# Two transformer blocks on one core: the last additions to x moved from the engines into accumulating transfers of GpSimd's queue

## The reference

```python
def second_block(x, ...):
    ...
        x = x + rms_norm(merged @ w_out[l], norm_mix_post[l])

        h = rms_norm(x, norm_ffn_pre[l])
        u = causal_dwconv(h @ w_up[l], conv_ffn_w[l])
        a, g = jnp.split(u, 2, axis=-1)
        f = (jax.nn.gelu(g, approximate=True) * a) @ w_down[l]
        x = x + rms_norm(f, norm_ffn_post[l])
    return x
```

## Time and profile before

| | us |
|---|---|
| median of 3 runs | 1413.34 |
| lowest and highest of them | 1412.82, 1951.74 |
| profiled execution, its own time | 1412.42 |
| profiled execution, its span | 1411.1 |
| PE busy in the span | 1362.0 |
| mean granted TensorE clock, share of full speed | 0.993 |

### The profile page before, as it was taken

The page is one execution under the profiler, slowest core; times in us unless marked ns, Lnnn a source line. Parts: engine busy times, 40 slices in busy tenths (PEclk is TensorE's granted clock), DMA queues, the critical chain, the costliest instruction groups (busy, mean ns, idle before and its releaser), DMA issues.

```text
span 1411.1 us, 17413 instructions
## 1 busy us (share of the span) xinstructions
PE 1362.0 (97%) x7040; PEld 1123.8 (80%) x7040; DVE 759.7 (54%) x1082; ACT 603.9 (43%) x866; POOL 7.0 (0%) x15
## 2 busy tenths in 40 slices
PE   5999998989999999999999999999989999999997
PEld 3777876878888888889888888788987888888886
DVE  5678855575555443335524444345767666563224
ACT  5646866453333333223334544334524443443221
POOL 0000000000000000000000000000000000000000
PEclk9999999999999999999999999999999999999998
DMA  9743321323332223323232121234302333323331
GB/s 382 274 136 135 128 72 57 129 78 138 143 135 94 100 86 98 95 82 103 79 101 75 60 75 47 75 106 146 106 16 80 100 92 106 101 86 98 95 95 60
DMA packets 43102, 150.45 MB, mean 107 GB/s; under 512 B 4752, under 2 KB 6928, under 8 KB 41872
## 3 DMA queue, kind: packets, MB, share of 16 engines
q1 hardware_dynamic: 42144, 144.76, 30.8%
q0 software_dynamic: 880, 4.59, 1.0%
HBM read 146.45 MB, written 2.10 MB: 105 GB/s over the span
## 4 chain that ended last, share of the span: by engine, by line
PE 87%; DVE 8%; ACT 3%; issue 2%; DMA 1%; DVEq 0%; SPq 0%; ACTq 0%
PE banks L580 26%; PE banks L582 25%; PE banks L581 25%; ACT w_hi L1321 1%; DVE w_lo L1871 1%; PE banks L865 1%; PE banks L724 1%; PE banks L732 1%; PE banks L721 1%; PE banks L1127 1%; PE banks L1126 1%; PE banks L848 1%; PE banks L694 1%; PE banks L1118 1%; PE banks L1154 1%
## 5 line engine op out<-in xcount | busy, mean ns | idle before, releaser
L580 PE MATMUL banks<-h_lo,w_hi 128*128 128x512 f32 (+1 forms) x1248 | 473.6, 380 | 13.1 <-DVE h_lo L2513 5.6
L582 PE MATMUL banks<-h_hi,w_hi 128*128 128x512 f32 (+1 forms) x1248 | 470.0, 377 | 0.0
L581 PE MATMUL banks<-h_hi,w_lo 128*128 128x512 f32 (+1 forms) x1248 | 469.3, 376 | 0.0
L1871 DVE TENSOR_TENSOR w_lo<-raw_w,w_hi 128x1024 fp32r<-128x1024 f32 (+2 forms) x221 | 256.2, 1161 | 322.2 <-ACT w_hi L1321 319.9
L1321 ACT ACTIVATE w_hi<-raw_w 128x1024 fp32r<-128x1024 f32 (+2 forms) x221 | 221.4, 1004 | 235.1 <-PE banks L582 210.1
L580 PEld LDWEIGHTS banks<-h_lo,w_hi 128*128 128x128 f32 x1248 | 234.3, 188 | 65.8 <-issue 10.5
L581 PEld LDWEIGHTS banks<-h_hi,w_lo 128*128 128x128 f32 x1248 | 234.5, 188 | 43.5
L582 PEld LDWEIGHTS banks<-h_hi,w_hi 128*128 128x128 f32 x1248 | 234.4, 188 | 42.4
L582 PE MATMUL banks<-a_hi,w_hi 128*128 128x512 f32 (+1 forms) x396 | 146.2, 369 | 0.0
L581 PE MATMUL banks<-a_hi,w_lo 128*128 128x512 f32 (+1 forms) x396 | 145.8, 368 | 0.0
L580 PE MATMUL banks<-a_lo,w_hi 128*128 128x512 f32 (+1 forms) x396 | 145.6, 368 | 0.0
(11 more groups left out here) (315 smaller groups left out, 1516.9 us busy)
## 6 DMA issues: line engine op xcount, KB each, us to landing
raw_w<-in_w_ffn_up SPq DMA_DIRECT2D x44, 512.0 KB, 3.4
raw_w<-in_w_up SPq DMA_DIRECT2D x44, 512.0 KB, 3.4
raw_w<-in_ada_rows SPq DMA_DIRECT2D x24, 512.0 KB, 4.2
early<-in_ada_turned SPq DMA_DIRECT2D x8, 1024.0 KB, 16.6
raw_w<-in_w_gates SPq DMA_DIRECT2D x16, 512.0 KB, 3.2
raw_w<-in_w_ffn_down SPq DMA_DIRECT2D x16, 448.0 KB, 3.3
raw_w<-in_w_down SPq DMA_DIRECT2D x16, 448.0 KB, 3.3
raw_w<-in_w_conv SPq DMA_DIRECT2D x12, 512.0 KB, 3.3
```

The source lines that it names most:

```text
L580: e.matmul(dst, lhs_hi, rhs_lo, start=first, stop=False)
L581: e.matmul(dst, lhs_lo, rhs_hi, start=False, stop=False)
L582: return e.matmul(dst, lhs_hi, rhs_hi, start=False, stop=last)
L1871: e.tensor_tensor(lo[:, 0:n], raw[:, i % RAW, 0:n], hi[:, 0:n].bitcast(F32), ALU.subtract).then_inc(s_lo, 1)
```

## The change

The last addition is no longer done by DVE and GpSimd.

- SP stores `x` as it is, unchanged since L2501, to the result in memory: four transfers of 512 KB, placed between the loads of the last `w_up` tile and of the first `w_down` tile.
- DVE only scales `y2_buf` by its factors, eight chunks in a row for each half.
- GpSimd waits once for the four stores of `x`. Then, for each pair of scaled chunks, it starts a transfer from `y2_buf` to the result that adds to what is there in memory (`accum_op=ALU.add`), 256 KB each, eight in all. Each is 128 partitions by 2 chunks by 256 positions, so 256 rows of 1 KB. They count on `s_out`, for which SP waits at the end, as before.

```diff
--- before.py
+++ after.py
@@ -421,8 +421,8 @@
 
 
 
-        s_c, s_cols, s_consts, s_crow, s_xc, s_sg_small, s_vmid, s_out = (
-            semaphore(f"in_{n}") for n in ("c", "cols", "consts", "crow", "xc", "sg_small", "vmid", "out"))
+        s_c, s_cols, s_consts, s_crow, s_xc, s_sg_small, s_vmid, s_residual, s_out = (
+            semaphore(f"in_{n}") for n in ("c", "cols", "consts", "crow", "xc", "sg_small", "vmid", "residual", "out"))
         s_bias = [semaphore(f"in_bias{i}") for i in range(2)]
         s_early = [semaphore(f"in_early{i}") for i in range(6)]
         s_x = [semaphore(f"in_x{i}") for i in range(KC // 2)]
@@ -2603,9 +2603,6 @@
                     y = y2_buf[:, k, tok]
                     e.scalar_tensor_tensor(out=y, in0=y, scalar=col("norm_ffn_post_2", k), in1=factors, op0=ALU.mult,
                                            op1=ALU.mult).then_inc(s_yn2.sem, 1)
-                    if k not in POOL_CHUNKS:
-                        e.wait_ge(*s_yn2.at(KC * half + k + 1))
-                        e.tensor_tensor(x[:, k, tok], x[:, k, tok], y, ALU.add).then_inc(s_x3_v.sem, 1)
 
         def gpsimd_program(e):
 
@@ -2627,11 +2624,12 @@
 
 
 
+            e.wait_ge(s_residual, 16 * KC // 2)
             for half in range(2):
-                for k in POOL_CHUNKS:
+                for k in range(1, KC, 2):
                     tok = HALVES[half]
                     e.wait_ge(*s_yn2.at(KC * half + k + 1))
-                    e.tensor_tensor(x[:, k, tok], x[:, k, tok], y2_buf[:, k, tok], ALU.add).then_inc(s_x3_p.sem, 1)
+                    e.dma_start(out[:, k - 1:k + 1, tok], y2_buf[:, k - 1:k + 1, tok], accum_op=ALU.add).then_inc(s_out, 16)
 
         def sync_program(e):
             def load(first, beyond):
@@ -2687,15 +2685,11 @@
             load_early(ADA_TILES + 2, ADA_TILES + 3)
             load(5, 6)
             load_early(ADA_TILES + 3, ADA_TILES + EARLY_ROWS // 2)
-            load(6, len(loads.load))
-            for half in range(2):
-                for k in range(1, KC, 2):
-                    for c in (k - 1, k):
-                        if c in POOL_CHUNKS:
-                            e.wait_ge(*s_x3_p.at(len(POOL_CHUNKS) * half + POOL_CHUNKS.index(c) + 1))
-                        else:
-                            e.wait_ge(*s_x3_v.at((KC - len(POOL_CHUNKS)) * half + c + 1 - sum(p < c for p in POOL_CHUNKS)))
-                    e.dma_start(out[:, k - 1:k + 1, HALVES[half]], x[:, k - 1:k + 1, HALVES[half]]).then_inc(s_out, 16)
+            load(6, loads.tile_load[W["down2"]])
+            e.wait_ge(s_x2_v, 2 * KC)
+            for k in range(0, KC, 2):
+                e.dma_start(out[:, k:k + 2, :], x[:, k:k + 2, :]).then_inc(s_residual, 16)
+            load(loads.tile_load[W["down2"]], len(loads.load))
             e.wait_ge(s_out, 16 * KC)
 
         tensor_program(nc.tensor)
```

## The result

The changed kernel took 1415.17 us (median of 20 runs) against 1412.75 us before. The ratio is 1.0015, with a 95% interval from 1.0008 to 1.0021: 1.1 to 3.0 us slower. The forecast was no change by the 2% bound, +0.3 us in all, with a range of 1410 to 1424. Its sign was right, its size too small. One execution of each kernel took far longer (1951.74 us before, 2282.06 us after) and is left out of the ratio.

What follows compares the result with a forecast made beforehand. PE bounds the kernel, busy 97% of the span, so only the tail after its last product could pay. DVE's 3.25 us off and the last step's 3.55 on gave +0.3, 1413.6 us by the median; range 1410.0 to 1424.

Steps and rivals of the forecast that it cites:

- DVE's part: In the tail, twelve additions go and the second half's reciprocal starts 0.08 us earlier: DVE ends 3.25 us sooner.
- The early stores at nothing: Stores of x ahead of the `w_down` loads: hidden by 2 to 8 us of cover before ACT, costed at nothing.
- Rival 5: Stores of x hold back the weights at `w_down`, at less than about 150 GB/s: 1418 at 110 GB/s; chance 0.03.
- The last step: From DVE's end to the span's end, accumulating GpSimd transfers replace SP's store: 2.35 becomes 5.90 us, 3.55 on.
- S: Time one 256 KB accumulating transfer holds the 16 DMA engines: taken as 1.5 us, bounds 0.75 and 22 us.
- completion after the last data: Last part of a transfer's landing in the tail, taken from the old stores' 2.3 us: 1.05 us.
- Rival 1: In the tail, adding costs the DMA engines nothing, S at most 1.0: 2.6 us sooner, 1410.7 by the median; chance 0.22.
- Rival 2: In the tail, adding is slower than doubling, by adder or descriptor writing: S = 2.5 gives +7.0 us; chance 0.22.
- the doubling: In the accumulating transfers, the old value is read too, so twice the bytes are read: S = 1.5 us.
- Rival 3: In the accumulating transfers, rows wait for each other: S = 22, 166 us later, 1580 us; chance 0.05.
- Rival 4: In the second half, DVE's scalings keep GpSimd from starting transfers: +2.7 us, 1416.0 by the median; chance 0.06.

Runs made afterwards that it cites:

- e2: Changed kernel with the eight transfers started from SP as plain stores, nothing added in memory: ratio to before 0.9983, reciprocal to end 6.54 us.
- e3: Kernel before with only the four early stores of x added: ratio to before 1.0002, reciprocal to end 9.82 us.
- e1: Changed kernel with the same eight transfers from GpSimd's queue as plain stores, without the adding: ratio to before 0.9986, reciprocal to end 7.67 us.
- e9: Changed kernel with the eight accumulating transfers aimed at x in SBUF instead of the result in memory: ratio to before 1.0005, reciprocal to end 10.95 us.
- e5: Changed kernel with result and y2_buf laid out by halves, eight transfers of 256 KB in rows of 2 KB: ratio to before 1.0027, reciprocal to end 11.51 us.
- e6: Changed kernel laid out by halves, four accumulating transfers of 512 KB in rows of 4 KB: ratio to before 1.0011, reciprocal to end 10.92 us.
- e7: Changed kernel accumulating only in the second half, first half added and stored as in the kernel before: ratio to before 1.0021, reciprocal to end 12.12 us.

## Why the prediction was nearly right

**DVE's part: right.** Summed at 3.17 us after the reciprocal, 3.23 in e2. The reciprocal ran 0.03 us after ACT's root, and the first half's saving gave nothing, as argued.

**The early stores at nothing: right in the outcome, wrong in one term.** SP's four issues were summed at 1.5 us and took 3.7. The tile was still 9 us ahead of ACT; e3 shows no cost. Rival 5 is out.

**The last step: right mechanism, S too small.** The prediction said that the last transfer waits for the three before it and not for DVE, and gave 1.43 us a transfer as the point at which the change stops paying. The engines were full as described, and S was 1.8 us where I took 1.5. This is the term that was mis-sized: four times 0.3 us is 1.2 us. Smaller terms miss as well. GpSimd began its issue 0.29 us after the scaling, for which the sum had nothing. The first data came 1.8 us after the issue, where I had 1.25: an issue takes 1.2 us and not 0.53. Against these, completion after the last data took about 0.4 us, where I had 1.05. With the measured values the sum closes to 0.1 us: 1403.71 + 1.8 + 4 x 1.8 + 0.4 = 1413.1, against 1413.2.

The 1.05 us came from a misreading. The first data of the old store don't stand in slice 8, near 1397.7, but in slices 10 and 11 of 0.1 us, near 1398.1. So SP's queue took 0.9 us to the first data and not 0.5, and 0.65 us are left for completion. GpSimd's start was then only 0.35 us later than SP's, and a plain store from it should have landed in 2.65 us, which is what the shortest of e1 did (2.7). The 3.0 agrees with e1's median only by luck, since the later stores of a half stood behind each other. By the right reading, S = 1.5 would have given 1404.35 + 6.0 + 0.65 = 1411.0, 0.1 us less than before: the forecast had its sign from this slip. The change would have stopped paying at S = 1.53. One bound is off too: S = 1.9 gives 1413.3 + 2.2 = 1415.5 by the median, and not 1415.8.

The ratio puts the loss at 2.1 us, the stretches at 1.87.

Why S was 1.8: e1 shows that it is the adding, e9 that it is mostly not HBM, e5 that it is neither GpSimd's issue nor a fixed time for a row, and e6 that twice the plain time is what remains with rows of 4 KB in transfers of 512 KB (1.54 against 0.78). That reading the old value makes the factor of two fits, but it isn't shown by itself: an adder with half the rate would look the same.

**The rivals.** Rival 1 (the adding is free) is what e1 would be. Rival 2 (slower than the doubling) was partly true: S was above 1.5 and just below the 1.82 from which the first half's transfers hold up the second's, and e7 shows that they didn't. GpSimd's issues did take longer than I had, as this rival has it, but e5 shows that they don't set the pace. Rival 3 (rows wait for each other) is out, at 1.8 us for 16 rows. Rival 4 (DVE keeps GpSimd from starting) is out: in e1 four issues of 0.72 us ran beside DVE's scalings.

The estimate from the Trainium skill, page "DMA: Bandwidth & Descriptors", section "Anatomy of one DMA — SWDGE (gpsimd) path", 2.6 us for 256 KB, is near the plain stores in e1, 2.7 us for the shortest and 3.0 in the median; it would have put the changed kernel 3 us faster, and the measurement decides against using it for a transfer that adds.

## What to carry to other kernels

An addition moved into a transfer is not free: here the DMA engines were held 2.5 times as long as by a plain store, and when several such transfers end the program their sum replaces the engine's time that was saved. Sum the engines' time of all transfers in the tail before comparing landings. One such transfer at the start of the tail can be hidden. Longer rows lower the engines' time for it, but rows of 2 KB didn't shorten this tail.

When a landing is taken apart, count the slices in the view: here 0.4 us too little before the first data and as much too much behind the last cancelled for the old queue, and not for the new one.

## What the runs showed of the hardware

- Accumulating transfers from GpSimd's queue: 1.98, 1.78 and 1.54 us of the 16 engines for 256 KB in rows of 1, 2 and 4 KB (summed over packets; 1.8 us of elapsed time with 1 KB); plain ones 0.78 us.
- Plain stores from GpSimd of the same 2048 rows of 1 KB show 640 packets in e1 where those from SP and the accumulating ones show 2176. Joined rows are one way to read this, four to a packet; the engines' time was the same as from SP.
- The issue on GpSimd takes 0.72 us plain. Accumulating, with 256 rows of 1 KB, it takes 1.17 us at the least and up to 2.67 us when issues overlap; with 128 rows of 2 or 4 KB 0.85 and 0.84 us at the least. The first data come some 0.6 us after the end of the first issue.
- An issue on GpSimd starts 0.3 us after its wait ends, 0.6 us for the first in the tail; an addition on GpSimd started 0.08 us after.
- SP's issue of four 512 KB stores in a row took 0.43 us at the least and 1.4 at the most.
